# First input stage without a copy of x, latents reloaded from the sync queue, and the third output product ahead of the sums of squares, in a one-core hybrid decoder layer

## The reference, cut to what matters

```
z = x @ w_in + b_in          # columns: GLU a, g | q latent 384 | kv latent 256 | rope key 64 | gates 2*1024
u = causal_dwconv(a * sigmoid(g), width 31);  y_conv = silu(layer_norm(u)) @ w_conv_out
q = rms_norm(z_q) @ w_uq ;   c_kv = rms_norm(z_kv);   k_rope = rope(z_kr)
y_mla = attention(q, c_kv, k_rope, paged caches) @ w_mla_out
mix = (sigmoid(gate_a) * y_conv + sigmoid(gate_b) * y_mla) @ w_mix_out
x1 = layer_norm(alpha * x + mix);   y = layer_norm(alpha * x1 + conv_ffn(x1))
```

## Time and profile before

| | |
|---|---|
| median of 3 runs | 2242.74 us (2235.79 to 2242.78) |
| the profiled execution | 2257.73 us, span 2255.9 us |
| PE busy | 2111.7 us, 94% of the span |
| DVE, ACT, POOL busy | 57%, 30%, 24% |
| chain that ended last | PE 70%, issue 13%, DVE 8%, POOL 3%, ACT 2%, DMA 2% |
| DMA | 182.78 MB, mean 81 GB/s |

### The profile page before, as it was taken

One profiled execution on the slowest core, in us unless ns is written; L12 is line 12 of the kernel. 1 busy time (PEld: TensorE's weight loads), 2 busy tenths in 40 slices (PEclk: granted clock), 3 DMA queues, 4 the chain that ended last, 5 costly groups with the idle time before them and its releaser, 6 DMA issues.

```text
span 2255.9 us, 34989 instructions
## 1 busy us (share of the span) xinstructions
PE 2111.7 (94%) x13793; PEld 1998.2 (89%) x13793; DVE 1279.5 (57%) x1748; ACT 666.7 (30%) x1107; POOL 535.6 (24%) x281
## 2 busy tenths in 40 slices
PE   5999999998989999979988999999999999999993
PEld 4999999997979888866657999899999999999992
DVE  5799999943546666634333324855445454454545
ACT  2222222243224444433332112522222122222212
POOL 2213343302100000033320134522222222222213
PEclk9999999999989999979997999999999999999995
DMA  7222232215310000046542442111111111111102
GB/s 234 77 87 82 85 113 85 87 46 196 125 41 13 12 23 12 19 163 234 190 178 95 143 108 89 31 54 46 40 47 38 47 41 53 46 37 52 45 25 99
DMA packets 163557, 182.78 MB, mean 81 GB/s; under 512 B 19838, under 2 KB 136376, under 8 KB 159303
## 3 DMA queue, kind: packets, MB, share of 16 engines
q1 hardware_dynamic: 144101, 102.36, 15.3%
q0 software_dynamic: 8368, 46.27, 5.4%
q10 hardware_dynamic: 10979, 32.68, 3.8%
HBM read 150.21 MB, written 31.93 MB: 81 GB/s over the span
## 4 chain that ended last, share of the span: by engine, by line
PE 70%; issue 13%; DVE 8%; POOL 3%; ACT 2%; DMA 2%; ACTq 1%; POOLq 0%; DVEq 0%; SPq 0%
PE psa L2006 21%; PE psb L2006 20%; PE psb L2160 5%; PE psa L2160 4%; PE psa L2546 4%; PE psb L2546 4%; POOL wlo L1363 3%; PE psb L2386 1%; PE pst L2365 1%; PE psa L2333 1%; PE psb L2333 1%; PE pst L2230 1%; DVE ptl L1612 1%; DMA gab<-ga_d 1%; DMA xt_d<-xst 1%
## 5 line engine op out<-in xcount | busy, mean ns | idle before, releaser
L1363 POOL TENSOR_TENSOR wlo<-wraw,whi 128x1024 fp32r<-128x1024 f32 x64 | 173.1, 2718 | 565.1 <-ACT whi L1167 565.1
L1444 DVE SCALAR_TENSOR_TENSOR pst<-g_ext,wtap,pst 128x512 f32<-128x512 f32 x464 | 306.9, 750 | 0.0
L1244 POOL TENSOR_TENSOR wlo<-wraw,whi 128x1024 fp32r<-128x1024 f32 x64 | 154.1, 2416 | 446.5 <-ACT whi L680 303.8
L1892 DVE TENSOR_SCALAR hg<-ueg,fwv,vec 128x1024 f32<-128x1024 f32 x22 | 19.3, 875 | 239.7 <-ACT ueg L1192 232.1
L2006 PE MATMUL psa<-x1h,whi 128*128 128x352 f32 x504 | 109.9, 326 | 3.5 <-POOL wlo L1363 2.0
L2006 PE MATMUL psa<-x1l,whi 128*128 128x352 f32 x504 | 109.1, 325 | 0.0
L2006 PE MATMUL psa<-x1h,wlo 128*128 128x352 f32 x504 | 109.0, 324 | 0.0
L2006 PE MATMUL psb<-x1h,whi 128*128 128x352 f32 x504 | 109.0, 324 | 0.0
L2006 PE MATMUL psb<-x1h,wlo 128*128 128x352 f32 x504 | 108.6, 323 | 0.0
L2006 PE MATMUL psb<-x1l,whi 128*128 128x352 f32 x504 | 108.5, 323 | 0.0
L1895 DVE SCALAR_TENSOR_TENSOR hg<-ueg,fwv,hg 128x1024 f32<-128x1024 f32 x44 | 97.0, 2204 | 5.7 <-DVE hg L1895 0.2
(11 more groups left out here) (472 smaller groups left out, 5450.8 us busy)
## 6 DMA issues: line engine op xcount, KB each, us to landing
wraw<-in_w_up SPq DMA_DIRECT2D x44, 512.0 KB, 3.8
wraw<-in_w_in SPq DMA_DIRECT2D x37, 512.0 KB, 3.8
wraw<-in_w_down SPq DMA_DIRECT2D x22, 512.0 KB, 3.5
gb_d<-stg ACTq DMA_DIRECT2D x8, 528.0 KB, 2.6
ga_d<-stg ACTq DMA_DIRECT2D x8, 528.0 KB, 3.8
gab<-ga_d ACTq DMA_DIRECT2D x8, 528.0 KB, 5.0
ma_d<-stg ACTq DMA_DIRECT2D x8, 528.0 KB, 2.9
tmp<-gb_d SPq DMA_DIRECT2D x8, 528.0 KB, 3.7
```

The costliest lines, as they stand in the source:

```text
L1244: nc.gpsimd.tensor_tensor(wlo[:, n % HL, :], wraw[:, n % RAW, :], whi[:, n % HL, :].bitcast(F32), ALU.subtract).then_inc(lo_done, 1)
L1363: nc.gpsimd.tensor_tensor(wlo[:, (ns + 2) % HL, :], wraw[:, (ns + 2) % RAW, :], whi[:, (ns + 2) % HL, :].bitcast(F32), ALU.subtract).then_ ...
L1444: half[x] = link(nc.vector.scalar_tensor_tensor(out=dst, in0=src, scalar=tap(k_), in1=pst[:, x, :], op0=ALU.mult, op1=ALU.add))
```

## The change

It does these things:

- **First stage.** The copy `xst` and POOL's nine writes are gone; the sum `stat` now releases the PSUM buffer. POOL makes x again as xh + xl into `tmp`, one tile of 128x1056 at a time (`x_tile`), eight of them, and writes them to `xt_d` during m = 0, 1 and 2, between its `lo` steps. The mean goes into `s1` in place of `tmp[0]`.
- **Order at the start.** SP issues the first weight load ahead of the last x rows, and the mask load after the state rows. PE makes product 0 first, and the tables between product 0 and product 1.
- **Last query block.** `read_z("q2")` stands in the swish loop at m = 5, behind the conv state and ahead of swish(6) and swish(7).
- **Latents.** SP, not ACT, reloads them: first gate tile 0, latents 0 to 4 in one DMA, gate tile 1, latent 5, then `cs`, each with the waits it needs, and all of it ahead of the load of weight block 2 of `w_conv_out`.
- **Sums of squares.** ACT's `after_ya(0)`, which splits the weights of ya2, comes ahead of the squares. DVE adds the squared tiles (three additions), so `skv` and `sq` are three float32 matmuls each. PE takes them after ya2 in place of before it; ACT and DVE follow that order.

```diff
@@ DVE and POOL, first stage
-                if t >= 2:
-                    dve.wait_ge(xt_out[t % 2], 16 * (t // 2))
-                nc.vector.tensor_copy(xst[t % 2][:, :, 0:n], src).then_inc(free[t % 2], 1)
+                nc.vector.reduce_sum(stat[:, t * P:t * P + n], src.rearrange("p k n -> p n k"), axis=AX.X
+                                     ).then_inc(free[t % 2], 1)
-            for t in range(9):
-                pool.wait_ge(free[t % 2], t // 2 + 2)
-                pool.dma_start(xt_d[:, :, t * P:t * P + n].rearrange("m p n -> p m n"), xst[t % 2][:, :, 0:n]
-                               ).then_inc(xt_out[t % 2], 16)
+            def x_tile(k):
+                if k >= 2:
+                    pool.wait_ge(xt_out[k % 2], 16 * (k // 2))
+                nc.gpsimd.tensor_tensor(tmp[k % 2][:, :], xh[:, k, :].bitcast(F32), xl[:, k, :].bitcast(F32), ALU.add
+                                        ).then_inc(x_sum, 1)
+                pool.wait_ge(x_sum, k + 1)
+                pool.dma_start(xt_d[k], tmp[k % 2][:, :]).then_inc(xt_out[k % 2], 16)
...
-                lo(4 * m + 2)
-                lo(4 * m + 3)
+                for t in range(2):
+                    lo(4 * m + 2 + t)
+                    if m < CSUM:
+                        for k in range(3 * m, min(MT, 3 * m + 3)):
+                            if (k > 3 * m) == (t == 1):
+                                x_tile(k)
@@ PE, first stage
+            def start_tables():
...
+            def in_products(m, past, between=None):
                 for t in range(4):
+                    if between is not None and t == 1:
+                        between()
...
-            with pe.Fori(0, CSUM) as m:
+            in_products(0, 0, start_tables)
+            with pe.Fori(1, CSUM) as m:
                 in_products(m, 0)
@@ SP
             for t in range(4, 9):
+                if t == 8:
+                    load(0, w_in_v[:, :, 0:P])
...
+            load(N1C, w_co_v[:, :, 0:P])
+            load(N1C + 1, w_co_v[:, :, P:2 * P])
+            sp.wait_ge(w_used, N1C + HL)
+            sp.wait_ge(stg_out[0], 16 * (MT + 4))
+            sp.dma_start(gab[0][:, :], ga_d[0]).then_inc(ga_in[0], 16)
+            sp.wait_ge(stg_out[1], 16 * (MT + 3))
+            sp.dma_start(zbuf[:, 0:5, :], z_d[0:5].rearrange("k p n -> p k n")).then_inc(z_in, 16)
+            sp.wait_ge(stg_out[1], 16 * (MT + 4))
+            sp.dma_start(gab[1][:, :], ga_d[1]).then_inc(ga_in[1], 16)
+            sp.dma_start(zbuf[:, 5, :], z_d[5]).then_inc(z_in, 16)
+            sp.dma_start(cs[:, :], A["c_rope"]).then_inc(cs_in, 16)
+            with sp.Fori(1, MT // 2) as i:
@@ ACT, third stage (read_z("q2") moved up, the reload and its waits gone)
             after_ya(0)
+            act.wait_ge(z_in, 32)
+            for k in range(5):
+                nc.scalar.activation(sqb[:, k, :], zbuf[:, k if k < 2 else k + 1, :], ACT.Square).then_inc(rms_sq, 1)
             after_ya(1)
+            after_ya(2)
             stat_read("skv", 2, rk[:, :], 1.0 / KL, RMS_EPS)
             stat_read("sq", 3, rq[:, :], 1.0 / QL, RMS_EPS)
-            after_ya(2)
@@ DVE and PE, third stage
+            for a, b in ((0, 1), (2, 3)):
+                dve.wait_ge(rms_sq, b + 1)
+                nc.vector.tensor_tensor(sqb[:, a, :], sqb[:, a, :], sqb[:, b, :], ALU.add).then_inc(rms_add, 1)
+            dve.wait_ge(rms_sq, 5)
+            dve.wait_ge(rms_add, 2)
+            nc.vector.tensor_tensor(sqb[:, 2, :], sqb[:, 2, :], sqb[:, 4, :], ALU.add).then_inc(rms_add, 1)
+            merge_a(2)
...
-            pe.wait_ge(rms_sq, 2)
-            column_sums(ready("skv"), [sqb[:, k, :] for k in range(2)])
-            pe.wait_ge(rms_sq, 5)
-            column_sums(ready("sq"), [sqb[:, k, :] for k in range(2, 5)])
+            weighed(N1C + 2, "ya2", sh, sl)
+            pe.wait_ge(rms_add, 1)
+            column_sums(ready("skv"), [sqb[:, 0, :]])
+            pe.wait_ge(rms_add, 3)
+            column_sums(ready("sq"), [sqb[:, 2, :]])
```

More of the change, by code:

```diff
@@ L372, in program @@
         xb_out = sem("x_mean_out")
+        x_sum = sem("x_tile_joined")
         xb_in = sem("x_mean_in")
@@ L412, in program @@
         for k, name in enumerate(("kv0", "kv1", "kr", "q0", "q1", "q2", "ya0", "ya1",
-                                  "skv", "sq", "ya2", "ya3", "ya4", "ya5", "ya6", "ya7")):
+                                  "ya2", "skv", "sq", "ya3", "ya4", "ya5", "ya6", "ya7")):
             take(name, k % 2)
@@ L506, in _, with load @@
                     sp.dma_start(ident[:, :], A["c_ident"]).then_inc(c_in, 16)
+            def load(n, src):
+                sp.wait_ge(lo_done, n + 1)
+                sp.dma_start(slot3(wraw, n % RAW), src).then_inc(raw_in[n % RAW], 16)
             for t in range(4, 9):
+                if t == 8:
+                    load(0, w_in_v[:, :, 0:P])
                 sp.wait_ge(x_hi, t - 3)
@@ L599, in _ @@
             sp.wait_ge(wm_out, 16 * MT)
+            for j in range(2):
+                sp.wait_ge(xt_out[j], 16 * (MT // 2))
             w_next(N3)
@@ L697, in _ @@
             act.wait_ge(stat_done, 1)
-            nc.scalar.activation(split(tmp[0][0:1, :]), psx[1][0:1, :, 0:CH], ACT.Copy, scale=1.0 / D).then_inc(free[1], 1)
+            nc.scalar.activation(split(s1[0:1, :]), psx[1][0:1, :, 0:CH], ACT.Copy, scale=1.0 / D).then_inc(free[1], 1)
             act.wait_ge(free[1], 6)
-            act.dma_start(xb_d, tmp[0][0:1, :]).then_inc(xb_out, 16)
+            act.dma_start(xb_d, s1[0:1, :]).then_inc(xb_out, 16)
             for r in range(4):
@@ L832, in _ @@
                                       ).then_inc(krow_out, 16)
[L833 to L845, removed]
+                    read_z("q2", 5, 1, V_Q + 2)
             def after_ya(m):
@@ L1269, in _ @@
                 lo(4 * m + 1)
+                if m == 0:
+                    pool.wait_ge(free[0], 6)
+                    pool.wait_ge(free[1], 5)
+                if m == CSUM:
+                    pool.wait_ge(xb_out, 16)
                 if m >= CSUM:
@@ L2060, in _ @@
             pe.wait_ge(free[1], 5)
-            def in_products(m, past):
+            def start_tables():
+                pe.wait_ge(v_in, 16 * 15)
+                nc.tensor.transpose(pst[:, 0, 0:V_ROWS], vrow[0:V_ROWS, :], ident[0:V_ROWS, 0:V_ROWS])
+                for h in range(2):
+                    n = CW * MT // 2
+                    nc.tensor.transpose(pst[:, 0, 128 + h * n:128 + (h + 1) * n], crow[0:n, h, :], ident[0:n, 0:n])
+                for h in range(2):
+                    n = FW * FT
+                    last = nc.tensor.transpose(pst[:, 0, 376 + h * n:376 + (h + 1) * n], frow[0:n, h, :], ident[0:n, 0:n])
+                last.then_inc(tr_done, 1)
+                pe.wait_ge(free[0], 6)
+                pe.wait_ge(free[1], 5)
+                column_sums(1, [stat])
+                pe.wait_ge(st_in, 16)
+                n = NB * HALO // 2
+                for r in range(4):
+                    if r:
+                        pe.wait_ge(tr_read, r)
+                    for mh in range(4):
+                        m, h = 2 * r + mh // 2, mh % 2
+                        last = nc.tensor.transpose(pst[:, (r + 1) % 2, mh * n:(mh + 1) * n],
+                                                   strows[:, h, m * P:(m + 1) * P], ident[0:n, 0:n])
+                    last.then_inc(tr_done, 1)
+            def in_products(m, past, between=None):
                 for t in range(4):
+                    if between is not None and t == 1:
+                        between()
                     pe.wait_ge(lo_done, 4 * m + (RAW + t + 1))
@@ L2144, in latent_rows @@
                                         ).then_inc(orow_t, 1)
-            for m in range(2, MT):
+            for m in range(3, MT):
                 weighed(N1C + m, f"ya{m}", sh, sl)
```

39 lines of the change are left out of this document (4 added, 35 removed).

## The result

The changed kernel takes 2224.36 us (median of 4 runs, 2222.12 to 2225.25) against 2240.47 (4 runs, 2235.79 to 2242.78); the ratio is 0.9922 [0.9903, 0.9941]. That is 16.1 us less, where 19.4 were forecast. Its profiled execution took 2224.38 us, with a span of 2222.6.

A forecast was written before the change was run, and what follows sets the result against it. PE bounds the second stage; the gain lies in two stretches where PE waits, the first 47.4 us and 535.2 to 564.5. 8.2 + 11.2 = 19.4 us off 2242.7 gives 2223.3; the range takes in 2219 and 2232.8.

The forecast's parts named there:

- Part 1: First stage, copy gone and product 0 ahead of the tables: product 1 starts 8.2 us earlier, bounds 6 to 12.
- The round of 5.56: First stage: one round of a PSUM buffer takes 5.56 us for two tiles without the copy, and is the bound.
- the half clock cost: Start of product 0 at the low level, 1.2 GHz: 1.9 us lost, taken from the sums at 542.
- the rival with the warm start: First stage: denser transposes lift the clock, 4 us more gained, 2219 us; chance 0.10.
- Part 2: POOL's eight additions beside the second stage: cost 0, bound 0 to 2.5 us lost.
- The bound's mechanism: Head of a conv: POOL's additions hold DVE's operations with both inputs in SBUF, once or twice 2.5 us.
- Part 3: Last query block ahead of swish(6) and swish(7): ya0 ends 1.9 us later, bounds 1.0 to 2.5.
- Part 4: Latents loaded by SP: ya2's weights ready at 534.6, ya2 can start at 537.0 with 2.4 us to spare.
- The rival with late weights: Ahead of ya2: weights queued behind 4.8 MB on SP come 7.6 us late, clock falls, 2232.8 us; chance 0.17.
- Part 5: Sums of squares behind ya2: ya3 starts at about 553.4, 11.2 us earlier, the 1.9 lost at ya0 included.
- The tail: Rival behind ya3: DVE's chain behind the reciprocals, or POOL's additions, cost 2 to 5 us, about 2227; chance 0.08.
- Sum, 19.4: Whole kernel: 8.2 from the first stage plus 11.2 at ya3, taken off the median 2242.7, gives 2223.3 us.

The follow-up runs named there:

- additions_twice: Changed kernel with each of POOL's eight additions (high plus low part of x) made twice; 2235.2 us, one profiled run.
- all_three_busy: Changed kernel with tables before product 0, last-query-block read behind seventh swish, ya2 weights before the latents wait, ten unread products before first-head scores; 2211.2 us (0.9870).
- the second comparison: The changed kernel, unedited, timed again against the kernel before on the same chip; 2221.2 us, ratio 0.9914.
- before_again: The kernel before, unchanged, run once more for its profile; 2241.9 us, one profiled run.

## Why the prediction was right, and where not

- **Part 1, 8.2 earlier: right, 8.04.** The round of 5.56 is exact, the ninth tile came at 26.17 (forecast 27.0), product 0 at 31.24 (31.9), product 1 at 51.17 (51.0). One term was mis-sized: the half clock cost 2.7, not 1.9, which had been read from a single case of twelve records. Over the eight traces with this first stage it cost 1.4 to 2.7, so 1.9 was a fair middle. The tables took 5.55 (5.5). No late x rows showed, but a part of the rival with the warm start did: the tile at 21.50 took 1.07 us, and that is why the ninth came 0.8 early; in additions_twice, where all eight full tiles took over 1.9, it came at 26.99. So near a hit as 51.17 is luck in part: 0.7 won ahead of product 0 and 0.8 lost in it. Behind the transposes the product began at 1.08 us a triple in place of 0.65. The Trainium skill (TensorE: Matmul & The Clock Gate, "Part 4: PE-mode transpose") has that transposes do not count as activity for the clock gate; the traces agree only in part. In the three traces that still have the copy all full tiles took 1.9 to 2.0, but in ten of the eleven without it, where less idle time lies between the tiles, one or two of the eight ran in 1.06 to 1.07, and the clock had fallen again before the work behind them.
  The prediction's own terms give 31.7 for product 0 (28.35 + 1.0 + 2.33), not 31.9, and 536.8 for the end of ya1, not 537.0; nothing hangs on either.
- **Part 2, nothing: right.** Doubled additions cost nothing either. The bound's mechanism, DVE held beside POOL, is real, 2.1 us once in the changed kernel's first convolution (a copy of 2.33 us in place of 0.18), and it lies in slack.
- **Part 3, 1.9 lost: right.** The two waits in the trace are 1.4 together, and putting the block back moved the first gate product by 1.9. The gain named there ("The z write goes out 4.6 earlier") was worth nothing, since that write then took 8.1 us to land, in place of 2.7.
- **Part 4, weights of ya2 with 2.4 to spare: wrong in the slack, right in the outcome.** They were 0.30 late, and PE waited for them, which the prediction names as a sign of being wrong. The step that failed is when SP gets to the rest, "at about 520": less the 8 us of the first stage that is 512, and SP got there at 515.71, when the z write had landed. The weights landed at 524.1 (forecast 531 - 8 = 523), and ya1 was over 1.5 us earlier than reckoned. The rival with late weights was close: up to 2.11 us in the five other traces with this part unedited, 2.44 where ya0 ran without waits.
- **Part 5, 11.2: right, 10.8.** From ya0's start to ya3's it was 564.56 - 511.50 = 53.06 and is 544.24 - 501.96 = 42.28. Of the remaining 1.5 of the 12.3, 1.3 came between c_mean and ya0 (46.9 before, 45.65 now). The change does not touch that work. It goes with the half clock there: 46.1 to 46.9 in the four traces with 6.8 us of it around c_mean, 45.5 to 45.7 in those with 3.4, and 44.1 in all_three_busy, which has none. The tail was not taken back: 20.1 at the start of attention.
- **Sum, 19.4: 20.1 reached, 3.4 given back** in the first head (44.04 against 40.65), which leaves 16.7; the medians say 16.1, and 19.0 in the second comparison (2240.24 against 2221.21). What the sum lacked was not a term of the change but the clock in a stage that had lost 3.2 us to it already and could lose 3.4 more. The prediction named clock trouble only at product 0 and in a gap ahead of ya2. That the time itself was met within 1.1 us (2223.3 forecast, 2224.36 measured) is luck in part: the median of 2242.7 that the sum was taken off stands 2.3 above that of the result's four runs, which hides most of what was given back.
- **The profiled execution of before** lay 15 us above its median. Its stretch from the first product with `wukT` to the first with `orw` took 205.4 us, in before_again 187.1 and in the changed kernel 188.9; on the chip where the kernel before takes 2258, four kernels show 199.2 to 203.9. What takes the time there is open. Taking the sum off the median and not off that execution was right.

## To carry to other kernels

When a stage ahead of the first product gets shorter, ask again which work fits the wait that is left: small jobs that need no weights belong into it, the more so as the half clock then falls on them. Moving a producer earlier brought nothing here, where its transfer fell beside a large read already under way; look at the landing, not at the issue. A short wait of PE ahead of heavy work can cost more than its own length, and unread products in it are a cheap trial.

## What had not been expected of the hardware

- A wait of 2.55 us was followed by half clock for 0, 6.8, 17.1 or 20.5 us, under a nearly always busy PE, at a price of up to 7.9 us (45.32 against 37.43). The first-head lengths fall on four values, 37.4 to 37.5, 40.6 to 40.7, 44.0 to 44.1 and 45.3, over at least three chips.
- The clock also fell without idle time. In the changed kernel 48 matmuls of a single column keep PE busy from 452.43 on, and the product behind them drops to 1.08 us a triple from 457.3 to 460.8:

```profile
454.26 2.02 PE L2120 MATMUL pst<-ones,tmp 128*88 128x1 f32 x24
456.14 0.73 PE L2141 MATMUL psb<-xh,whi 128*128 128x352 f32 x3
456.70 0.83 PE L2141 MATMUL psb<-xl,whi 128*128 128x352 f32 x3
457.33 1.08 PE L2141 MATMUL psb<-xh,wlo 128*128 128x352 f32 x3
```

  It fell around there in thirteen of the fourteen traces, for 3.4 or 6.8 us. In all_three_busy it did not, which is the 1.6 us at its first merge. That the narrow matmuls bring it about was not tested.
- A write of 528 KB took 8.12 us to land behind a read of 2640 KB issued 4.0 us earlier, and 3.52 when issued 8.5 us after it.
- With less idle time between the transposes a tile or two of them ran at full clock (1.07 in place of 1.94 us); before the first product the clock had fallen again.
- Beside POOL's addition of 128x1056 a DVE copy of 32 columns took 2.33 us in place of 0.18, and ended with it.
